# Input loaded first, parameter stage merged into the GLA stage, first norm's weight spread by a TensorE product into PSUM

## The chip, the cores and the metric

The kernel runs on one core of a Trainium2 chip. The metric is the device time of one execution in microseconds (us); the time of a kernel is the median of its runs. The engines are TensorE (PE, its weight loads PEld), VectorE (DVE), ScalarE (ACT), GpSimd (POOL) and SyncE (SP), which issues the DMAs. SBUF is the on-chip memory, PSUM the memory that TensorE writes its results to.

## What is computed

Two blocks of a language model in a row, fp32, on one sequence of 1024 rows of width 1024. The change lies in the very first steps: the first RMS norm of the input and the gate projection behind it.

```python
def first_block(x, mix_norm_w, ...):
    h = rmsnorm(x, mix_norm_w[0])
    x = x + gla_mixer(h, gla_w_in, gla_w_gate2, gla_b_gate, gla_norm_w, gla_w_out)
    h = rmsnorm(x, ffn_norm_w[0])
    x = x + conv_ffn(h, ffn_w_up, ffn_conv_w, ffn_conv_b, ffn_w_down)
    return rmsnorm(x, final_norm_w)

def second_block(x, ...):        # the output of the first block
    x = x + hybrid_mixer(rms_norm(x, norm_mix), ...)
    x = x + jnp.square(jax.nn.relu(rms_norm(x, norm_mlp) @ w_up)) @ w_down
    return rms_norm(x, norm_final)
```

rmsnorm divides each row of x by the root of its mean square and multiplies it by a weight vector of length 1024. In gla_mixer (gated linear attention, 4 heads), h is multiplied with one wide matrix that holds the keys, queries, values, the output gate and a decay gate of rank 16.

## The kernel before

The program is a sequence of stages: parameters (L902), gla (L955), gated_ffn, hybrid, square_ffn. Each ends in end_stage (L890): semaphores are cleared and all engines meet at a barrier (L893). Within a stage each engine runs its own instruction list, ordered by semaphores. fp32 products are made of three matmuls on high and low parts (product, L131): high times high, high times low, low times high. So every operand is split into two tensors.

**parameters** loads an identity matrix (L912), then 14 small tensors of per-channel parameters as rows (L914 to L933), then the 8 row tiles of x (128x1024 each, 512 KB, L936), all on SP's queue. TensorE turns the rows into columns in PSUM (L944) when all of them are there; VectorE copies them to c.par (L951) and also sets c.zero, a column of zeros. Later stages read c.par; within gla the first readers are the gate's absolute value on ACT (L1212) and its counterpart on VectorE (L1278).

**gla** starts on SP with the norm's weight row, which the load spreads over all 128 partitions into the tile gla_q (L1035), and the 128 columns of the weight matrix that hold the gate (graw, in gla_y, L1036). Then follow, in the order of a list of phases, the second gate weight (L1043) and the tiles of the wide matrix (st.load, L109), each after the first two waiting for a free raw buffer. GpSimd splits graw into high and low parts (L1063, L1066) and then each weight tile (L125, L128), into four slots; the fifth tile waits until TensorE has used a slot.

The norm (class Norm, L184) goes over the 8 tiles m, in an order that Lags (L745) writes out. ACT: square of tile k (L200), root of tile k-1 (L211), high part of tile k-4 (L238). VectorE: variance of tile k-1 (L206), scaling of tile k-2 (reciprocal L216, then L225: X times the reciprocal root times the weight row, into one of two buffers in gla_v), low part of tile k-4 (L245, from PSUM and SBUF). TensorE: turning of each scaled tile by 8 transposes (L232) into PSUM DD or MM; it waits for the scaled tile and for the low part two tiles earlier. A scaling waits for the turning two tiles earlier, and the first one for the weight row (L218).

After tile 7 TensorE makes the gate product (L1097, 48 matmuls of 128x512 into MM), ACT copies it (L1200), TensorE makes the first gate of head 0 (L1128), and then the key tile (k.0), and so on through the phases, by head.

Of the kernel before, what the change touches and what calls it, by code (L numbers as in the profile page):

```python
# [15 lines left out]
ACT = mybir.ActivationFunctionType  # L16
AX = mybir.AxisListType.X
F32 = mybir.dt.float32
# [5 lines left out]
P = 128  # L24
SEQ = 1024
D = 1024
MT = SEQ // P
DOWN = 2 * MT
KT = D // P
HALF = 512  # L30
# [7 lines left out]
FT = FFN_DIM // P  # L38
# [18 lines left out]
C_END = C_NM + 8  # L57
# [126 lines left out]
class Norm:  # L184
# [3 lines left out]
    def __init__(self, sem, name, core, xn, junk, row, pairs, ready):  # L188
        self.core, self.xn, self.junk, self.row, self.ready = core, xn, junk, row, ready
        self.pairs = pairs  # L190
        self.row_in, self.squared, self.vars, self.roots, self.scaled, self.turned, self.hi, self.lo = (
            sem(f"{name}_{s}") for s in ("row_in", "squared", "var", "root", "scaled", "turned", "hi", "lo"))
# [20 lines left out]
    def scale(self, dve, m):  # L213
# [3 lines left out]
        if m == 0:  # L217
            dve.wait_ge(self.row_in, 16)  # L218
# [512 lines left out]
class RowNorm(Norm):  # L731


    def __init__(self, sem, name, core, junk, row, ready):
        self.core, self.junk, self.row, self.ready = core, junk, row, ready
# [91 lines left out]
class Program:  # L827
# [74 lines left out]
    def parameters(self):  # L902
        nc, c, a = self.nc, self.core, self.a
        with ExitStack() as ctx:
            rows = ctx.enter_context(nc.sbuf_tensor("param_rows", [P, 3, P], F32))[:]
            s_rows, s_id, s_turn, s_par = (self.sem(n) for n in ("rows_in", "ident_in", "params_turned", "params_ready"))
            last = C_END - 2 * ROWS
            block = ctx.enter_context(nc.Block())

            @block.sync  # L910
            def _(sp):
                sp.dma_start(c.ident, a["ident"]).then_inc(s_id, 16)  # L912
                taps = a["ffn_conv_w"][0].rearrange("t (f p) -> (t f) p", p=P)
                sp.dma_start(rows[0:ROWS, 0, :], taps[0:ROWS, :]).then_inc(s_rows, 16)  # L914
                sp.dma_start(rows[0:2 * FT, 1, :], taps[ROWS:3 * 2 * FT, :]).then_inc(s_rows, 16)
                sp.dma_start(rows[2 * FT:ROWS, 1, :],
                             a["ffn_conv_b"][0].rearrange("(f p) -> f p", p=P)).then_inc(s_rows, 16)
                n = 0
                for src in (
                    a["gla_b_gate"][0].rearrange("(f p) -> f p", p=P),  # L920
                    a["gla_norm_w"][0].rearrange("(f p) -> f p", p=P),
                    a["conv_w_2"][0].rearrange("t (f p) -> (t f) p", p=P),
                    a["conv_b_2"][0].rearrange("(f p) -> f p", p=P),
                    a["b_r_2"][0].rearrange("(f p) -> f p", p=P),
                    a["b_i_2"][0].rearrange("(f p) -> f p", p=P),
                    a["lam_2"][0].rearrange("(f p) -> f p", p=P),
                    a["hg_norm_2"],
                    a["lb_logits_2"][0].rearrange("(f p) -> f p", p=P),
                    a["ffn_norm_w"][0].rearrange("(f p) -> f p", p=P),
                    a["norm_mlp_2"][0].rearrange("(f p) -> f p", p=P),  # L930
                ):
                    k = src.shape[0]
                    sp.dma_start(rows[n:n + k, 2, :], src).then_inc(s_rows, 16)  # L933
                    n += k
                for m in range(MT):
                    sp.dma_start(c.X[:, m, :], a["x"][0, m * P:(m + 1) * P, :]).then_inc(self.x_in[m], 16)  # L936

            @block.tensor
            def _(pe):
                pe.wait_ge(s_id, 16)  # L940
                pe.wait_ge(s_rows, 16 * 14)
                for g in range(3):
                    k = ROWS if g < 2 else last
                    mm = pe.transpose(c.MM[:, g * ROWS:g * ROWS + k], rows[0:k, g, :], c.ident[0:k, 0:k])  # L944
                mm.then_inc(s_turn, 1)

            @block.vector
            def _(dve):
                dve.memset(c.zero, 0.0)
                dve.wait_ge(s_turn, 1)  # L950
                dve.tensor_copy(c.par, c.MM[:, 0:C_END]).then_inc(s_par, 1)  # L951
                dve.wait_ge(s_par, 1)


    def gla(self, following):  # L955
# [6 lines left out]
        with ExitStack() as ctx:  # L962
# [26 lines left out]
            def at(h, name):  # L989
# [13 lines left out]
                "y_hi", "y_lo", "down_mm", "down_add")}  # L1003
            scratch = V.rearrange("p (b m) v -> p b (m v)", b=2)
            norm = Norm(self.sem, "gla_norm", c, scratch, T1, Q, (c.DD, c.MM), lambda m: (self.x_in[m], 16))
# [83 lines left out]
            def _(pe):  # L1089
                pe.sem_inc(st.used, 1)  # L1090
                head.tensor(pe, lambda m: None)
                pe.wait_ge(norm.lo, MT)
# [7 lines left out]
                pe.wait_ge(s["glr"], 1)  # L1100

# [95 lines left out]
            def _(act):  # L1197
# [1459 lines left out]
```

## Time and profile before

| | us |
|---|---|
| median of 3 runs | 2998.28 |
| the runs | 2997.21 to 3000.92 |
| the profiled execution | 2997.87 |
| its span in the trace | 2995.1 |
| TensorE busy | 2807.6 (94%) |
| VectorE busy | 1550.7 (52%) |
| GpSimd busy | 1624.7 (54%) |
| ACT busy | 1044.1 (35%) |

The profile is that of one execution. Its span starts with the first and ends with the last recorded instruction; the execution's own time is 2.8 us longer. Times in the rows are microseconds from the span's start unless marked ns. SPq is a DMA issue on SP. A row of the timeline gives start, duration, engine, line, operation, the tile written and the tiles read, the count of merged instructions, and in brackets how long the engine had been idle before and which event ended that. The granted clock of TensorE is given as a share of 2.4 GHz.

### The profile page before, as it was taken

The numbers are of one execution on the slowest core, as the hardware profiler recorded it, in microseconds if no ns is written. First come the engines' busy times: TensorE is split into PE (matmuls) and PEld (weight loads), VectorE is DVE, ScalarE is ACT, GpSimd is POOL, SyncE is SP. The second block draws the span as 40 slices with busy tenths as digits, with TensorE's granted clock in tenths as the row PEclk, the third lists the DMA queues.
The fourth block names the chain that finished last, engine by engine and source line by source line (L and its number), as shares of the span: only waits on it lengthen the run. The fifth ranks groups of instructions, "written<-read, shape, count | busy, mean of one in ns | idle before, by whom it ended". The sixth has DMA issues, their size and how long they took to land. (4 is left out here: it accounts for less than half of the span.)

```text
span 2995.1 us, 38841 instructions
## 1 busy us (share of the span) xinstructions
PE 2807.6 (94%) x13675; PEld 2323.1 (78%) x13675; DVE 1550.7 (52%) x1972; ACT 1044.1 (35%) x1484; POOL 1624.7 (54%) x1096
## 2 busy tenths in 40 slices
PE   5999997799999999589999999999998999999998
PEld 4888786688888887467777777777777788888886
DVE  4233425355555555846566566566444344444445
ACT  3213215333333333434444444443524222222222
POOL 3332333577677765665465465565433656555552
PEclk8999998899999999799999999999999999999999
DMA  3110110121111112111121121111250111111112
GB/s 115 36 50 28 42 42 0 35 57 54 51 49 56 56 49 70 60 46 35 54 61 33 56 60 32 57 57 36 77 190 8 50 49 56 56 56 45 46 49 84
DMA packets 200853, 160.62 MB, mean 54 GB/s; under 512 B 6246, under 2 KB 176827, under 8 KB 200763
## 3 DMA queue, kind: packets, MB, share of 16 engines
q1 hardware_dynamic: 200763, 159.35, 17.6%
q8 instruction: 64, 1.05, 0.1%
q14 instruction: 26, 0.21, 0.0%
HBM read 143.60 MB, written 15.73 MB: 53 GB/s over the span
## 5 line engine op out<-in xcount | busy, mean ns | idle before, releaser
L312 POOL TENSOR_TENSOR w_lo<-w_raw,w_hi 128x512 fp32r<-128x512 f32 x280 | 393.6, 1412 | 310.1 <-ACT w_hi L306 309.9
L408 PE MATMUL PA<-h_hi,w_hi 128*128 128x512 f32 x840 | 352.6, 420 | 61.1 <-ACT hy_gm L2338 19.9
L409 PE MATMUL PA<-h_lo,w_hi 128*128 128x512 f32 x840 | 340.1, 405 | 0.0
L410 PE MATMUL PA<-h_hi,w_lo 128*128 128x512 f32 x840 | 339.3, 404 | 0.0
L312 POOL TENSOR_TENSOR w_lo<-f_sums,w_hi 128x512 fp32r<-128x512 f32 x114 | 168.5, 1478 | 168.8 <-ACT w_hi L306 168.8
L306 ACT CAST w_hi<-w_raw 128x512 fp32r<-128x512 f32 x280 | 168.7, 616 | 245.4 <-DMA w_raw<-in_w_in 115.8
L408 PEld LDWEIGHTS PA<-h_hi,w_hi 128*128 128x128 f32 x840 | 166.0, 198 | 104.4 <-issue 35.1
L408 PE MATMUL PB<-f_t_hi,w_hi 128*128 128x512 f32 x560 | 220.9, 395 | 1.7 <-ACT hy_tm L2341 0.9
L410 PE MATMUL PB<-f_t_hi,w_lo 128*128 128x512 f32 x560 | 218.3, 390 | 0.0
L409 PE MATMUL PB<-f_t_lo,w_hi 128*128 128x512 f32 x560 | 217.9, 389 | 0.0
L312 POOL TENSOR_TENSOR w_lo<-w_lo_raw,w_hi 128x512 fp32r<-128x512 f32 x108 | 140.4, 1307 | 128.9 <-ACT w_hi L306 128.9
L409 PEld LDWEIGHTS PA<-h_lo,w_hi 128*128 128x128 f32 x840 | 166.5, 198 | 37.2 <-issue 3.6
L410 PEld LDWEIGHTS PA<-h_hi,w_lo 128*128 128x128 f32 x840 | 165.4, 197 | 36.7
L362 POOL TENSOR_TENSOR w_raw<-w_raw,params 128x1024 f32<-128x1024 f32 x76 | 143.0, 1903 | 77.1 <-DMA w_raw<-in_ffn_w_up 50.2
L312 POOL TENSOR_TENSOR w_lo<-hy_ring_sums,w_hi 128x512 fp32r<-128x512 f32 x96 | 137.2, 1429 | 70.6 <-ACT w_hi L306 70.6
L134 PE MATMUL DD<-w_hi,f_a_hi 128*128 128x512 f32 x416 | 162.9, 392 | 4.7 <-POOL w_lo L312 4.7
L135 PE MATMUL DD<-w_lo,f_a_hi 128*128 128x512 f32 x416 | 162.8, 391 | 0.0
L136 PE MATMUL DD<-w_hi,f_a_lo 128*128 128x512 f32 x416 | 162.8, 391 | 0.0
L134 PE MATMUL MM<-w_hi,f_a_hi 128*128 128x512 f32 x416 | 162.1, 390 | 0.0
L135 PE MATMUL MM<-w_lo,f_a_hi 128*128 128x512 f32 x416 | 162.0, 389 | 0.0
L136 PE MATMUL MM<-w_hi,f_a_lo 128*128 128x512 f32 x416 | 161.8, 389 | 0.0
L125 POOL TENSOR_TENSOR w_hi<-w_raw,params 128x1024 fp32r<-128x1024 f32 x24 | 48.4, 2016 | 192.3 <-PE PB L136 86.1
(469 smaller groups left out, 7139.1 us busy)
## 6 DMA issues: line engine op xcount, KB each, us to landing
w_raw<-in_w_in SPq DMA_DIRECT2D x64, 512.0 KB, 5.3
w_raw<-in_ffn_w_up SPq DMA_DIRECT2D x44, 512.0 KB, 4.6
w_raw<-in_w_up SPq DMA_DIRECT2D x32, 512.0 KB, 5.3
w_lo_raw<-in_w_down SPq DMA_DIRECT2D x64, 256.0 KB, 2.5
w_raw<-in_gla_w_in SPq DMA_DIRECT2D x24, 512.0 KB, 3.7
w_lo_raw<-in_ffn_w_down SPq DMA_DIRECT2D x44, 256.0 KB, 2.6
X<-in_x SPq DMA_DIRECT2D x8, 512.0 KB, 6.6
w_raw<-in_gla_w_out SPq DMA_DIRECT2D x8, 512.0 KB, 3.5
```

Of the source, the lines that this page charges most:

```text
L125: pool.tensor_tensor(hi, raw, self.core.zero[:, 0:1].broadcast_to([P, UNIT]), ALU.add)\
L134: pe.matmul(out, ah, bh, start=first, stop=False)
L135: pe.matmul(out, ah, bl, start=False, stop=False)
L136: return pe.matmul(out, al, bh, start=False, stop=last)
L306: act.copy(self.slot(i, p)[0], source).then_inc(self.hi_done, 1)
L312: pool.tensor_tensor(lo, source, hi.bitcast(F32), ALU.subtract).then_inc(self.split, 1)
L362: pool.tensor_tensor(raw, raw, column.unsqueeze(2).broadcast_to([P, KT, P]), ALU.mult)\
L408: pe.matmul(bank, ah[:, k, :], bh[:, k, :], start=(k == 0 and not more), stop=False, skip_group_check=more)
L409: pe.matmul(bank, ah[:, k, :], bl[:, k, :], start=False, stop=False, skip_group_check=more)
L410: mm = pe.matmul(bank, al[:, k, :], bh[:, k, :], start=False, stop=(k == 3), skip_group_check=more)
```

## The change

The stage parameters goes away, with its barrier. SP now begins, in the gla stage, with the norm's weight row as one row of 4 KB in one partition, then x tile 0, the identity, x tiles 1 to 7, graw, the 14 small parameter loads, and then the phases as before. TensorE multiplies a row of 128 ones with the weight row, in two products of 512 columns, into the PSUM tile PA; the scalings read the weight row there. The turning of the parameters stands on TensorE between the norm's turnings and the gate product, in PB; the copy to c.par stands on VectorE after the norm. ACT takes one root of a zero before anything else. TensorE and ACT wait for the copy before the first gate; GpSimd and ACT wait for the column of zeros, which VectorE now sets in this stage. T2, T3 and Q of the stage, free until later, hold the rows, the weight row and the ones.

```diff
@@ class Norm @@
         if m == 0:
-            dve.wait_ge(self.row_in, 16)
+            dve.wait_ge(*(self.row_ready or (self.row_in, 16)))
@@ parameters() becomes load_parameters(): the same 14 loads, no barrier @@
-            def _(sp):
-                sp.dma_start(c.ident, a["ident"]).then_inc(s_id, 16)
...
-                for m in range(MT):
-                    sp.dma_start(c.X[:, m, :], a["x"][0, m * P:(m + 1) * P, :]).then_inc(self.x_in[m], 16)
...
+    def load_parameters(self, sp, rows, arrived):
+        a = self.a
+        taps = a["ffn_conv_w"][0].rearrange("t (f p) -> (t f) p", p=P)
+        sp.dma_start(rows[0:ROWS, 0, :], taps[0:ROWS, :]).then_inc(arrived, 16)
...
+            k = src.shape[0]
+            sp.dma_start(rows[n:n + k, 2, :], src).then_inc(arrived, 16)
+            n += k
@@ gla, tiles @@
+            param_rows = T2[:, 0:3 * P].rearrange("p (g n) -> p g n", g=3)
+            mix_row, ones = T3[0:1, :], Q[0:1, 0:P]
-            norm = Norm(self.sem, "gla_norm", c, scratch, T1, Q, (c.DD, c.MM), lambda m: (self.x_in[m], 16))
+            norm = Norm(self.sem, "gla_norm", c, scratch, T1, c.PA, (c.DD, c.MM), lambda m: (self.x_in[m], 16))
+            norm.row_ready = s["mix_row"], 1
@@ gla, sync @@
-                sp.dma_start(norm.row, a["mix_norm_w"][0].partition_broadcast(P)).then_inc(norm.row_in, 16)
+                sp.dma_start(mix_row, a["mix_norm_w"]).then_inc(s["mix_in"], 16)
+                for m in range(MT):
+                    sp.dma_start(c.X[:, m, :], a["x"][0, m * P:(m + 1) * P, :]).then_inc(self.x_in[m], 16)
+                    if m == 0:
+                        sp.dma_start(c.ident, a["ident"]).then_inc(s["ident_in"], 16)
                 sp.dma_start(graw, W[:, :, GLA_IN - P:GLA_IN]).then_inc(s["graw_in"], 16)
+                self.load_parameters(sp, param_rows, s["rows_in"])
@@ gla, gpsimd @@
                 pool.wait_ge(s["graw_in"], 16)
+                pool.wait_ge(s["zero"], 1)
@@ gla, tensor @@
+                pe.wait_ge(s["mix_in"], 16)
+                pe.wait_ge(s["ones"], 1)
+                for half in range(2):
+                    cols = slice(half * HALF, (half + 1) * HALF)
+                    mm = pe.matmul(c.PA[:, cols], ones, mix_row[:, cols], start=True, stop=True)
+                mm.then_inc(s["mix_row"], 1)
+                pe.wait_ge(s["ident_in"], 16)
                 head.tensor(pe, lambda m: None)
+                pe.wait_ge(s["rows_in"], 16 * 14)
+                for g in range(3):
+                    k = ROWS if g < 2 else C_END - 2 * ROWS
+                    mm = pe.transpose(c.PB[:, g * ROWS:g * ROWS + k], param_rows[0:k, g, :], c.ident[0:k, 0:k])
+                mm.then_inc(s["params_turned"], 1)
                 pe.wait_ge(norm.lo, MT)
...
                 pe.wait_ge(s["glr"], 1)
+                pe.wait_ge(s["params"], 1)
@@ gla, scalar @@
+                act.wait_ge(s["zero"], 1)
+                act.activation(qo[:, 0:1], c.zero, ACT.Sqrt)
                 head.scalar(act)
                 act.wait_ge(s["glr_mm"], 1)
                 act.copy(GLR, c.MM).then_inc(s["glr"], 1)
+                act.wait_ge(s["params"], 1)
@@ gla, vector @@
+                dve.memset(ones, 1.0).then_inc(s["ones"], 1)
+                dve.memset(c.zero, 0.0).then_inc(s["zero"], 1)
...
                 head.vector(dve, lambda m: None)
+                dve.wait_ge(s["params_turned"], 1)
+                dve.tensor_copy(c.par, c.PB[:, 0:C_END]).then_inc(s["params"], 1)
+                dve.wait_ge(s["params"], 1)
@@ build @@
-        p.parameters()
-        p.end_stage()
         p.gla(stream_of("f1", p.f1_ring))
```

## Rows read from the trace of the kernel before

**Rows 1.** page, slices: TensorE's busy tenths in 40 equal slices

```profile
PE   5999997799999999589999999999998999999998
```

**Rows 2.** waits of TensorE to 110 us: waiter, releaser: total, times, longest

```profile
PE DD L232 <- DVE gla_v L225: 13.5, 1, 13.5
```

**Rows 3.** timeline from the start

```profile
0.76 0.39 SPq L912 DMA_DIRECT2D ident<-in_ident  x1
...
6.10 3.86 SPq L936 DMA_DIRECT2D X<-in_x  x8
...
7.38 0.69 PE L944 MATMUL MM<-ident,param_rows 88*128 88x88 f32 x3 [7.38 <-DMA param_rows<-in_norm_mlp]
...
10.77 0.33 SPq L1035 DMA_DIRECT2D gla_q<-in_mix_norm_w  x1
...
11.63 5.14 SPq L1043 DMA_DIRECT2D gla_gate<-in_gla_w_gate  x1
```

**Rows 4.** from issue to landing: x tiles, weight row (gla_q), identity (size, us)

```profile
DMA to landing us min/median/max: 3.7/6.6/9.3
DMA to landing us min/median/max: 9.4/9.4/9.4
ident<-in_ident SPq DMA_DIRECT2D x1, 64.0 KB, 1.9
```

**Rows 5.** timeline, first squares on ACT and first scalings on VectorE

```profile
12.07 1.06 ACT L200 ACTIVATE gla_t<-X 128x1024 f32<-128x1024 f32 x1
...
13.32 1.06 ACT L200 ACTIVATE gla_t<-X 128x1024 f32<-128x1024 f32 x1
...
20.25 1.28 DVE L225 SCALAR_TENSOR_TENSOR gla_v<-X,rs,gla_q 128x1024 f32<-128x1024 f32 x1 [4.07 <-DMA gla_q<-in_mix_norm_w]
...
23.59 2.27 DVE L225 SCALAR_TENSOR_TENSOR gla_v<-X,rs,gla_q 128x1024 f32<-128x1024 f32 x1 [0.43 <-PE DD L232]
```

**Rows 6.** timeline of the norm under way, VectorE and GpSimd

```profile
30.49 1.50 DVE L225 SCALAR_TENSOR_TENSOR gla_v<-X,rs,gla_q 128x1024 f32<-128x1024 f32 x1
30.99 3.22 POOL L128 TENSOR_TENSOR w_lo<-w_raw,w_hi 128x1024 fp32r<-128x1024 f32 x1
...
31.91 1.21 DVE L245 TENSOR_TENSOR h_lo<-DD,h_hi 128x1024 fp32r<-128x1024 f32 x1
...
33.33 1.96 DVE L225 SCALAR_TENSOR_TENSOR gla_v<-X,rs,gla_q 128x1024 f32<-128x1024 f32 x1
```

**Rows 7.** L225 grouped (busy us, mean ns); L1319 by source (ns min/median/max)

```profile
L225 DVE SCALAR_TENSOR_TENSOR gla_v<-X,rs,gla_q 128x1024 f32<-128x1024 f32 x8 | 13.8, 1720 | 4.9 <-DMA gla_q<-in_mix_norm_w 4.1 <-PE DD L232 0.4
L1319 DVE SCALAR_TENSOR_TENSOR gla_y_lo<-MM,params,gla_y_hi x6: 1275/1283/1284, 160.6 to 382.8; 128x1024 fp32r<-128x1024 f32 x6
```

**Rows 8.** timeline, GpSimd's first and last early operation, and the norm's end

```profile
21.99 2.79 POOL L1063 TENSOR_TENSOR gla_y_hi<-gla_y,params 128x1024 fp32r<-128x1024 f32 x1 [21.52 <-DMA gla_y<-in_gla_w_in]
...
39.40 2.02 DVE L225 SCALAR_TENSOR_TENSOR gla_v<-X,rs,gla_q 128x1024 f32<-128x1024 f32 x1
...
42.69 1.94 PE L232 MATMUL MM<-ident,gla_v 128*128 128x128 f32 x8 [1.35 <-DVE h_lo L245]
...
46.99 0.79 PE L134 MATMUL MM<-h_hi,gla_y_hi 128*128 128x512 f32 x1 [2.36 <-DVE h_lo L245]
...
47.52 2.38 POOL L128 TENSOR_TENSOR gla_w_lo<-w_raw,gla_w_hi 128x1024 fp32r<-128x1024 f32 x1
```

**Rows 9.** timeline behind the product; windows (busy us, PEclk, DMA share, GB/s)

```profile
61.44 1.98 PE L1128 MATMUL DD<-gla_glr,gla_gate 128*128 128x512 f32 x4 [1.10 <-ACT gla_glr L1200]
...
62.86 0.80 PE L134 MATMUL PA<-h_hi,w_hi 128*128 128x512 f32 x1
30.00:40.00 10.00, 6.42 (x27) 5.34 (x28) 9.70 (x15) 5.37 (x9) 9.84 (x4) 0.50 0.17 52
51.00:52.00 1.00, 1.00 (x4) 0.84 (x3) 0.00 (x0) 0.00 (x0) 0.00 (x0) 0.65 0.79 147
```

**Rows 10.** waits of TensorE from 62 to 500 us, the largest group

```profile
PE MM L1117 <- DVE gla_y L1273: 7.4, 4, 1.9
```

More of the change, by code:

```diff
@@ L190, in __init__ @@
         self.pairs = pairs
+        self.row_ready = None
         self.row_in, self.squared, self.vars, self.roots, self.scaled, self.turned, self.hi, self.lo = (
@@ L734, in __init__ @@
     def __init__(self, sem, name, core, junk, row, ready):
-        self.core, self.junk, self.row, self.ready = core, junk, row, ready
+        self.core, self.junk, self.row, self.ready, self.row_ready = core, junk, row, ready, None
         self.row_in, self.squared, self.vars, self.roots, self.scaled = (
@@ L900, in h_tiles @@
                 for x in (c.hhi, c.hlo)]
[L902 to L910, printed above, removed]
-            def _(sp):
-                sp.dma_start(c.ident, a["ident"]).then_inc(s_id, 16)
[L913 to L934, printed above, removed]
-                for m in range(MT):
-                    sp.dma_start(c.X[:, m, :], a["x"][0, m * P:(m + 1) * P, :]).then_inc(self.x_in[m], 16)
[L938 to L952, printed above, removed]
@@ new lines, in load_parameters @@
+    def load_parameters(self, sp, rows, arrived):
+        a = self.a
+        taps = a["ffn_conv_w"][0].rearrange("t (f p) -> (t f) p", p=P)
+        sp.dma_start(rows[0:ROWS, 0, :], taps[0:ROWS, :]).then_inc(arrived, 16)
+        sp.dma_start(rows[0:2 * FT, 1, :], taps[ROWS:3 * 2 * FT, :]).then_inc(arrived, 16)
+        sp.dma_start(rows[2 * FT:ROWS, 1, :], a["ffn_conv_b"][0].rearrange("(f p) -> f p", p=P)).then_inc(arrived, 16)
+        n = 0
+        for src in (
+            a["gla_b_gate"][0].rearrange("(f p) -> f p", p=P),
+            a["gla_norm_w"][0].rearrange("(f p) -> f p", p=P),
+            a["conv_w_2"][0].rearrange("t (f p) -> (t f) p", p=P),
+            a["conv_b_2"][0].rearrange("(f p) -> f p", p=P),
+            a["b_r_2"][0].rearrange("(f p) -> f p", p=P),
+            a["b_i_2"][0].rearrange("(f p) -> f p", p=P),
+            a["lam_2"][0].rearrange("(f p) -> f p", p=P),
+            a["hg_norm_2"],
+            a["lb_logits_2"][0].rearrange("(f p) -> f p", p=P),
+            a["ffn_norm_w"][0].rearrange("(f p) -> f p", p=P),
+            a["norm_mlp_2"][0].rearrange("(f p) -> f p", p=P),
+        ):
+            k = src.shape[0]
+            sp.dma_start(rows[n:n + k, 2, :], src).then_inc(arrived, 16)
+            n += k
@@ L1002, in gla @@
                 "r", "kdt_mm", "kdt", "st_mm", "s", "o_mm", "o_sq", "o_ms", "o_sd", "o_n", "y", "yt_mm",
-                "y_hi", "y_lo", "down_mm", "down_add")}
+                "y_hi", "y_lo", "down_mm", "down_add", "ident_in", "mix_in", "ones", "mix_row", "rows_in",
+                "params_turned", "params", "zero")}
+            param_rows = T2[:, 0:3 * P].rearrange("p (g n) -> p g n", g=3)
+            mix_row, ones = T3[0:1, :], Q[0:1, 0:P]
             scratch = V.rearrange("p (b m) v -> p b (m v)", b=2)
-            norm = Norm(self.sem, "gla_norm", c, scratch, T1, Q, (c.DD, c.MM), lambda m: (self.x_in[m], 16))
+            norm = Norm(self.sem, "gla_norm", c, scratch, T1, c.PA, (c.DD, c.MM), lambda m: (self.x_in[m], 16))
+            norm.row_ready = s["mix_row"], 1
             head = Lags(None, norm)
```

## The prediction

> **What bounds the kernel now.** I began with the shares by engine and their forty slices [rows 1]: TensorE is busy for 94% of the span and from the second slice on hardly leaves it, but the first slice (75 us) has a 5. The change touches only that slice, so everything is read there. TensorE's waits up to 110 us [rows 2] are led by 13.5 us for the first normalised tile. The start of the timeline [rows 3] shows why. SP issues the identity and 14 small parameter loads first, so the first tile of x is issued at 6.10; TensorE turns the parameters at 7.38; a barrier follows; and only at 10.77 is the norm's weight row requested, a load of 512 KB spread over all partitions, behind 4 MB of x in the same queue. It takes 9.4 us to land, a tile of x 3.7 to 9.3 us [rows 4]. So VectorE's first scaling starts at 20.25 with three tiles already squared, on the event "weight row landed" [rows 5]. From there the norm runs tile by tile on VectorE, which is full: one scaling (L225), one low half (L245) and two tiny operations each [rows 6]. The last low half releases the gate product of 48 matmuls at 46.99 [rows 8]. After that TensorE waits for nothing that keeps its own time: up to 500 us its largest group of waits sums to 7.4 us, for VectorE, and none is for a DMA or GpSimd [rows 10]. The path is therefore: load order, weight row, eight tiles on VectorE, gate product, TensorE to the end. What the product's start moves, the end moves.
>
> **Part 1, start of the chain.** SP starts at 0.76. An issue of a tile takes 3.86/8 = 0.48 us and of a small load about 0.35 (15 issues from 0.76 to 6.10) [rows 3]. After the change the order is weight row (0.76), x tile 0 (1.13), identity, x tiles 1 to 7. Tile 0 landed 3.7 us after its issue [rows 4], so now at 4.85. The last landed 9.3 us after an issue at 9.5, at 18.8; that is 1.29 us a tile. Tile 1, behind the 64 KB identity, comes at 6.3, tile 2 at 7.6, tile 7 at 14.0. ACT takes 1.25 us for a square [rows 5]: square 0 ends at 6.1, square 1 at 7.6, root 0 at 7.8. The loop lets VectorE scale tile 0 after the variance of tile 1, so at 8.05 instead of 20.25: **12.2 us earlier**. Next it waits for TensorE's turning of tile 0, as before: 20.25 to 23.59 is 3.34 us [rows 5], so the third scaling starts at 11.4.
>
> What must be there by 8.05 and is new: the weight row in PSUM. Its 4 KB load is issued at 0.76; the 64 KB identity landed 1.9 us after its issue [rows 4], so about 2.7. The two products on a row of ones are not in the trace; the nearest rows are the gate's own two fp32 products of 128x512, 1.98 us together at full clock [rows 9], at the lower clock about double. They end at 4.7 to 6.7, at least 1.3 us before they are needed: nothing on the path, and a microsecond for each that the row is late beyond that. The memset of ones and zeros are below 0.2 us each, before 2 us. ACT's root of a zero, with the table load that it brings, runs while ACT would stand idle until tile 0 lands at 4.85: nothing.
>
> **Part 2, the eight scalings.** By the grouped row they took 13.8 us, 1.72 each, though the shortest took 1.28 [rows 7]: 3.5 us of excess. The timeline says where it is. At 30.49 VectorE starts a scaling (X and weight row both in SBUF); GpSimd's operation before 30.99 is just ending; the scaling lasts 1.50. The GpSimd operation that starts at 30.99 lasts 3.22, against 2.38 when VectorE is idle, and the next scaling, from 33.33, lasts 1.96 [rows 6, 8]. The low halves, which read one operand from PSUM, take 1.21 in the same stretch [rows 6]. So two SBUF operands on VectorE and GpSimd's work wait for each other. Now the weight row is read from PSUM: 1.28 us each, the figure of the same kind of operation with one operand in PSUM, L1319 [rows 7]. Bounds: 0 us (the wait stays) to 3.5 us gained; I take **3.5 us**, because L1319 and L245 are nearest. From the third scaling on a tile then costs 2.84 - (1.50 - 1.28) = 2.62 us [rows 6]. The rest of the loop has room: TensorE turns a tile in 1.94 at the lower clock [rows 8], ACT needs about 1.0 for the high half and 1.25 for the square, 2.3 with the root. x arrives every 1.29 us, so it is not late again.
>
> The Trainium skill, page "SBUF — State Buffer", section "Who interferes with whom", says that a VectorE instruction with two SBUF inputs and a GpSimd instruction that reads SBUF exclude each other for the whole instruction, and that with at most one SBUF input there is no contention. By that rule, the trace agrees: the 3.22 and the 1.96 are each a whole wait plus an unslowed operation. The Trainium skill, page "VectorE: DVE Perf Modes", section on the TRN2 errata, speaks against the change: 120 fixed cycles with a PSUM source against 58, an estimated 0.065 us a scaling, 0.5 us in all. L1319's 1.28 us with a PSUM operand equals the scaling's 1.28 from SBUF, so the row does not bear it out and the sum leaves it out.
>
> **Part 3, the end of the norm.** Before, from the start of the eighth scaling (39.40) to the product (46.99) are 7.59 us: scaling 2.02, low half, turning 1.94, high half, low half [rows 8]. With 1.28 it is 6.85. New: third scaling 11.4, five steps of 2.62, eighth scaling 24.5, product at 31.35. Against 46.99 that is **15.6 us** earlier (12.2 + 3.5, less rounding).
>
> **Part 4, the parameters moved in behind.** SP issues the load of graw and then the 14 small ones at 0.35 us: 5.9 to 10.8, landing behind x and graw, some 5 MB at 0.41 MB/us from 3.6 on: by about 16. If the queue holds them as it held L1043's issue, 5.14 us [rows 3], by 21. TensorE waits for them after the last turning, which ends at about 28.9: its three small transposes (0.7 us, as at 7.38 [rows 3]) fit in the 2.3 us in which it waits for the last low half anyway. VectorE copies 128x277 in 0.45 us after its last low half, beside the 13 us of the product; ACT and TensorE want the result only behind the product. Cost: nothing while that cover stands, up to 0.7 + 0.45 us without it. The barrier and the old stage cost nothing more, they are inside the 20.25.
>
> Also behind the small loads are the gate weights and the first two weight tiles, 11 to 16.8. GpSimd gets graw at about 15.6 (21.99 before) and needs two halves and four weight tiles, 27.9 us in all (21.99 to 49.90 [rows 8]), less where VectorE no longer blocks it: done by 44 at the latest, by 49 if those loads are 5 us late. TensorE takes the first weight tile at about 47 instead of 62.8 [rows 9] and it is split by 27 to 32. Cost nothing; after this GpSimd waits for TensorE's slots as before.
>
> **Part 5, clock.** TensorE's granted clock was at its lower level in the second half of the norm (0.50, 1.2 GHz) and rose to the upper one (2.4 GHz) between 51 and 52 us, about 4.4 us into the product that had kept TensorE busy without a gap since 46.99 [rows 8, 9]. I expect the same: 11 matmuls at 0.43 us instead of 0.23, worth 2.2 us. It is the same cost on both sides. Bounds: the clock is already high (2.2 us gained) or rises later, by about as much lost.
>
> **Sum.** Profiled execution: span 2995.1, time 2997.87. Less 15.6: span 2979.5, time 2982.3. The median of the runs shown is 0.4 us above the profiled one: **2982.7 us**.
>
> **Rivals.**
> (a) The wait between VectorE and GpSimd stays although the row is in PSUM, or PSUM operands are slower: 2 to 3.5 us less gain, 2984.7 to 2986.2. For: the trace has no operation with exactly the second operand in PSUM beside a busy GpSimd. Against: L245 under the same GpSimd stretch.
> (b) The chain's start is later than I say: the row's load plus two products at the lower clock, or a slower first landing in a cold queue. 1 to 4 us less gain, 2983.7 to 2986.7.
> (c) The clock stays high into the product, since the turnings are now closer together: 2.2 us more, 2980.5.
> (d) Slower: the small parameter loads. TensorE stands in order in front of the product until all 14 have landed. If SP's queue, full of 4.6 MB, held each as long as L1043's load, 5.14 us, they would land near 80 and the product would start 33 us later than before: 3031 us. It costs from a landing at about 29 on, makes the kernel no faster from 46.3, and slower by over 0.2% from 52.3. Against: the eight x tiles were issued without any such hold [rows 3] and data drain by 16.
> (e) The gain is absorbed: a queue half as bad, landing at 40 to 52, gives within 0.2%.
>
> **Chances.** Forecast 0.62, own range 2980.0 to 2984.7; (a) 0.10; (b) 0.13; (c) 0.07; other faster outcomes 0.02; (e) 0.04; (d) 0.02. A measurement of this kernel tells about 0.2%, 6 us, from no change. Faster 0.94, same 0.04, slower 0.02. The range leaves out (d), (e) and half of the extremes: 2979.5 to 2988.
>
> **What would show it.** Right: first scaling near 8, eight scalings at 1.28 us, product near 31.3, no wait of TensorE for parameters, GpSimd's four early weight operations near 1.9 and 2.4 us, and from the product on the old timeline shifted by 15 to 16 us. Wrong: a first scaling released by the weight row in PSUM (b); scalings near 1.7 (a); TensorE waiting for a parameter load (d, e); a different granted clock in the product (c); a new TensorE wait for GpSimd behind 47 us.

## The result, and the profile after the change

The changed kernel takes 2979.56 us (median of 4 runs, 2976.03 to 2984.49) against 2998.9 us (4 runs, 2997.21 to 3000.92); the ratio is 0.994, 95% interval 0.9925 to 0.9954. In two further comparisons the same kernel gave 2980.30 us against 2999.03 us, ratio 0.9943 (0.9929 to 0.9956), and 2981.78 us against 2996.86 us, ratio 0.9953 (0.9939 to 0.9966). Over all 14 runs its median is 2980.3 us. The profiled execution is the slowest of its four: 2984.49 us, span 2982.7.

TensorE's slices now begin with a 7, where before they began with a 5 [rows 1]; of the other 39 digits one has changed, by one.

```profile
PE   7999997899999999589999999999998999999998
```

The start of the timeline after the change. The product on ones (L1078) answers to the load of the weight row [rows 3], L226 is the scaling that was L225 [rows 5 and 6], L1046 and L1049 are GpSimd's splitting of graw [rows 8].

```profile
2.20 3.77 PE L1078 MATMUL PA<-gla_t,gla_q 1*128 1x512 f32 x4 [2.20 <-DMA gla_t<-in_mix_norm_w]
...
6.96 5.17 SPq L907 DMA_DIRECT2D gla_t<-in_ffn_conv_w  x1
7.74 1.06 ACT L201 ACTIVATE gla_t<-X 128x1024 f32<-128x1024 f32 x1 [1.77 <-DMA X<-in_x]
...
9.25 1.28 DVE L226 SCALAR_TENSOR_TENSOR gla_v<-X,rs,PA 128x1024 f32<-128x1024 f32 x1
...
12.66 1.28 DVE L226 SCALAR_TENSOR_TENSOR gla_v<-X,rs,PA 128x1024 f32<-128x1024 f32 x1 [0.51 <-PE DD L233]
...
15.28 1.28 DVE L226 SCALAR_TENSOR_TENSOR gla_v<-X,rs,PA 128x1024 f32<-128x1024 f32 x1
...
17.37 1.89 POOL L1046 TENSOR_TENSOR gla_y_hi<-gla_y,params 128x1024 fp32r<-128x1024 f32 x1 [16.91 <-DMA gla_y<-in_gla_w_in]
...
19.34 2.36 POOL L1049 TENSOR_TENSOR gla_y_lo<-gla_y,gla_y_hi 128x1024 fp32r<-128x1024 f32 x1
```

What to see: the weight row is in PSUM at 5.97 (2.20 plus 3.77) and nobody waits for it. The first scaling starts at 9.25 instead of 20.25, directly behind square and root of tile 1, which ACT could start only at 7.74 because x tile 1 had not landed. Every scaling takes 1.28 us, and GpSimd's operations take 1.89 and 2.36 us beside them. SP is held for 5.17 us at the first small load.

The end of the norm and the product, with rows that answer to [rows 8 and 9]:

```profile
25.69 1.28 DVE L226 SCALAR_TENSOR_TENSOR gla_v<-X,rs,PA 128x1024 f32<-128x1024 f32 x1
...
28.26 1.94 PE L233 MATMUL MM<-ident,gla_v 128*128 128x128 f32 x8 [0.62 <-DVE h_lo L246]
...
29.99 0.67 PE L1085 MATMUL PB<-ident,gla_t 88*128 88x88 f32 x3
...
32.42 0.44 DVE L1256 COPY params<-PB 128x277 f32<-128x277 f32 x1
...
32.56 0.79 PE L134 MATMUL MM<-h_hi,gla_y_hi 128*128 128x512 f32 x1 [1.90 <-DVE h_lo L246]
...
38.27 0.48 PE L135 MATMUL MM<-h_lo,gla_y_hi 128*128 128x512 f32 x1
...
46.50 1.01 ACT L1198 COPY gla_glr<-MM 128x1024 f32<-128x1024 f32 x1 [15.25 <-PE MM L136]
...
48.98 0.80 PE L134 MATMUL PA<-h_hi,w_hi 128*128 128x512 f32 x1
```

The product starts at 32.56 (before 46.99: 14.4 us earlier), the copy behind it at 46.50 (before 60.38: 13.9 us earlier), the first key tile at 48.98 (before 62.86: 13.9). The three transposes of the parameters lie inside the wait for the last low half, and the copy of the parameters beside the product's first matmuls. TensorE's waits up to 110 us, to be read beside [rows 2]: the 13.5 us for the first scaled tile are 4.7, and no row names a parameter load.

```profile
PE DD L233 <- DVE gla_v L226: 4.7, 1, 4.7
...
PE PA L1078 <- DMA gla_t<-in_mix_norm_w: 2.2, 1, 2.2
```

### The profile page after: what moved, and what is told of

It reads as the page before. It is cut to its first block and busy times, and to the rows that moved or that the text cites. A ratio compares the mean times of both kernels' runs of the same rounds, so it can differ in the third digit from the quotient of the medians.

```text
span 2982.7 us, 38829 instructions
## 1 busy us (share of the span) xinstructions
PE 2813.7 (94%) x13679; PEld 2325.7 (78%) x13679; DVE 1545.7 (52%) x1973; ACT 1042.7 (35%) x1484; POOL 1619.8 (54%) x1096
## 3 DMA queue, kind: packets, MB, share of 16 engines
q1 hardware_dynamic: 200621, 158.83, 17.6%
```

## The experiments

In all of them the gate product's start and the start of ACT's copy behind it are read as the two marks of the path (46.99 and 60.38 in the kernel before, 32.56 and 46.50 in the changed one). Kernels are compared with runs of the kernel before on the same chip.

### The changed kernel again

No edit.

> The changed kernel once more, nothing edited. It is to separate the change from the spread between executions. Theory (the start alone moved): gate product starts at 32 to 33 us, as in the changed kernel's profile (32.56), and any difference in the whole time lies in single stretches of lower granted clock in the GLA heads (there were three of 3.4 us up to 400 us in the changed kernel's profile, one in the profile of before). Median 2977 to 2983. Rival (something later waits for a weight or a parameter): the same extra TensorE waits in every execution at the same place, median near 2984.

Measured: 2980.30 us (5 runs, 2979.64 to 2985.21), ratio 0.9943 (0.9929 to 0.9956). Product at 32.35, copy at 45.76. The profiled execution has a span of 2977.9, 4.8 us less than the first one of the same kernel, though its copy starts only 0.7 us earlier. Windows of TensorE in the three places where the first execution had fallen to the lower clock (columns: the window and its length, busy us and counts of PE, PEld, DVE, ACT, POOL, then the granted clock, the DMA share and GB/s), first of that execution, then of this one:

```profile
120.00:135.00 15.00, 13.09 (x76) 8.90 (x75) 7.57 (x22) 5.78 (x15) 7.30 (x4) 0.89 0.09 34
228.00:246.00 18.00, 16.18 (x92) 11.03 (x89) 10.30 (x22) 8.39 (x17) 9.34 (x4) 0.91 0.10 30
340.00:357.00 17.00, 15.18 (x77) 10.16 (x76) 10.90 (x18) 10.09 (x16) 9.34 (x4) 0.90 0.17 47
```

```profile
120.00:135.00 15.00, 13.10 (x81) 9.54 (x80) 8.26 (x21) 7.98 (x15) 8.04 (x4) 1.00 0.10 35
228.00:246.00 18.00, 16.17 (x85) 11.23 (x84) 11.32 (x20) 10.60 (x18) 9.34 (x4) 0.91 0.17 46
340.00:357.00 17.00, 15.19 (x79) 11.39 (x78) 12.84 (x20) 12.13 (x16) 9.37 (x4) 1.00 0.21 62
```

The clock is below 1.00 in three windows there and in one here. These are stretches of 3.4 us at 1.2 GHz. In the first execution they start at 130.6, 239.8 and 349.1 us, one head (109 us) apart, each within 1.1 us of the end of a wait of TensorE for VectorE of 1.8 to 1.9 us. The second execution has the same three waits, but only one such stretch, at 238.4. Summed over the record of the granted clock behind 60 us, TensorE was at the lower clock for 181.5 us in the first execution and for 174.7 in this one. At half the clock a busy engine loses half of the time, so I take half of the 6.8 us, 3.4, as an estimate; with the 0.7 us of the start this makes 4.1 of the 4.8. TensorE's large waits behind 62 us are the same in both (7.4 us for L1277's result in the one and 7.3 in the other), so nothing new is late.

### The weight row read from SBUF

```diff
-            norm = Norm(..., scratch, T1, c.PA, (c.DD, c.MM), ...)
-            norm.row_ready = s["mix_row"], 1
+            norm = Norm(..., scratch, T1, Q, (c.DD, c.MM), ...)
+            norm.row_ready = s["row_copied"], 1
@@ vector, ahead of the norm @@
+                dve.wait_ge(s["mix_row"], 1)
+                dve.tensor_copy(Q, c.PA).then_inc(s["row_copied"], 1)
```

> The changed kernel, but VectorE first copies the spread weight row from PSUM to SBUF, and the scalings read it there. Theory (VectorE with two SBUF operands and GpSimd exclude each other): the scalings before GpSimd's first operation (17.4 us) stay at 1.28 us, the four after it take 1.5 to 2.0, GpSimd's early operations 2.9 and 3.2 instead of 1.9 and 2.4; product starts 2 to 3 us later than 32.6, at 34.5 to 35.6. Rival (PSUM has nothing to do with it; the earlier start alone avoids GpSimd): eight scalings at 1.28 and the product at 32.6 as in the changed kernel.

```profile
17.19 2.48 DVE L226 SCALAR_TENSOR_TENSOR gla_v<-X,rs,gla_q 128x1024 f32<-128x1024 f32 x1
...
18.67 3.22 POOL L1049 TENSOR_TENSOR gla_y_lo<-gla_y,gla_y_hi 128x1024 fp32r<-128x1024 f32 x1
...
21.02 1.96 DVE L226 SCALAR_TENSOR_TENSOR gla_v<-X,rs,gla_q 128x1024 f32<-128x1024 f32 x1
...
34.68 0.79 PE L134 MATMUL MM<-h_hi,gla_y_hi 128*128 128x512 f32 x1 [1.90 <-DVE h_lo L246]
```

Measured: 2985.15 us (4 runs, 2984.47 to 2985.54), ratio 0.9952 (0.9937 to 0.9967). Four scalings at 1.28 us, then, from GpSimd's first operation at 16.70 on, 2.48, 1.96, 1.50 and 2.02; product at 34.68. The 2.48 is above the 1.5 to 2.0 that I expected, and GpSimd's first operation took 1.89 and not 2.9: it had begun before the fifth scaling, which waited for it. The first scaling was early here (7.82), so the stretch from it to the product is the fair measure: 26.86 us against 23.31 in the first profile of the changed kernel and 24.05 in the second. The 2.84 us over four scalings (7.96 less 4 times 1.28) lie on the path. The rival, that the earlier start alone avoids GpSimd, is out: it does so for the first four tiles only.

### The weight row as a spreading load, behind x

```diff
-                sp.dma_start(mix_row, a["mix_norm_w"]).then_inc(s["mix_in"], 16)
@@ behind the eight x tiles @@
+                sp.dma_start(norm.row, a["mix_norm_w"][0].partition_broadcast(P)).then_inc(norm.row_in, 16)
@@ tensor @@
-                (the wait for mix_in and ones, and the two products)
```

> The changed kernel, but without the product on ones: the weight row comes again as a load that spreads it over 128 partitions (512 KB), behind the eight x tiles. Theory (the first scaling waited for this load, x alone gives little): first scaling at 15.5 to 17 us, released by that load; scalings again 1.28 to 2.3 us beside GpSimd; product at 41.5 to 43.5 us; total 4 to 6 us under the kernel before. Rival (x's early arrival is the gain, the row only rides along): first scaling near 9.3, product near 35, total 10 or more us under the kernel before.

```profile
15.99 1.28 DVE L226 SCALAR_TENSOR_TENSOR gla_v<-X,rs,gla_q 128x1024 f32<-128x1024 f32 x1 [7.93 <-DMA gla_q<-in_mix_norm_w]
...
42.75 0.80 PE L134 MATMUL MM<-h_hi,gla_y_hi 128*128 128x512 f32 x1 [1.90 <-DVE h_lo L246]
```

Measured: 2993.69 us (10 runs, 2988.40 to 2997.84), ratio 0.9987 (0.9977 to 0.9996). The edit also takes the scalings' weight row back into SBUF. VectorE stood idle for 7.93 us until the row landed at 16; the scalings were 1.28 to 2.20 us again; product at 42.75, 4.2 us earlier than before. With x first and the stages merged, but the row in its old form and place, most of the gain is missing. A spreading load issued ahead of x, with no product on TensorE, was not tried.

### The weight row alone

The kernel before with the 4 KB load in the old place, the product on ones, and the scalings from PSUM; the parameter stage stays.

```diff
-                sp.dma_start(norm.row, a["mix_norm_w"][0].partition_broadcast(P)).then_inc(norm.row_in, 16)
+                sp.dma_start(mix_row, a["mix_norm_w"]).then_inc(s["mix_in"], 16)
@@ tensor, ahead of the norm @@
+                (the two products into PA, as in the change)
```

> The kernel before with one part of the change: the weight row is a 4 KB load, spread by the product on ones into PSUM and read there; the parameter stage, its barrier and the load order stay. Theory (the row's place behind x decides when it comes, its size hardly): it lands with the last x tile near 19, TensorE needs 3.4 to 3.8 us for the two products at the lower clock, first scaling at 22 to 23, but eight scalings at 1.28 us, product at 45.5 to 46.5, total 0 to 2 us under the kernel before. Rival (the spreading load of 512 KB is what delays the first scaling): first scaling at 15 to 18, product at 38 to 42, total 5 to 9 us under it.

```profile
18.62 3.78 PE L1098 MATMUL PA<-gla_t,gla_q 1*128 1x512 f32 x4 [10.60 <-DMA gla_t<-in_mix_norm_w]
...
22.52 1.28 DVE L226 SCALAR_TENSOR_TENSOR gla_v<-X,rs,PA 128x1024 f32<-128x1024 f32 x1 [6.31 <-PE PA L1098]
...
45.61 0.50 PE L134 MATMUL MM<-h_hi,gla_y_hi 128*128 128x512 f32 x1 [2.36 <-DVE h_lo L246]
```

Measured: 2995.45 us (10 runs, 2988.34 to 2996.85), ratio 0.9989 (0.9979 to 0.9998). The 4 KB, requested at 10.80, landed at 18.6 with the last of x; TensorE then took 3.78 us for the two products, so the first scaling is 2.3 us later than before. The eight scalings at 1.28 us win it back and 1.4 us more, although GpSimd works beside them from 20.56 on. The median fell by 3.7 us against the kernel before on its chip, more than the 0 to 2 that I expected; the profiled execution fell by 1.8. The size of the row's load matters little, its place in the queue much: in this place 4 KB took 7.8 us to land and 512 KB took 9.4 [rows 4], at the front 4 KB took 1.44.

### x first, with two stages

```diff
@@ parameters() @@
+                for m in range(MT):
+                    sp.dma_start(c.X[:, m, :], a["x"][0, m * P:(m + 1) * P, :]).then_inc(self.x_in[m], 16)
                 sp.dma_start(c.ident, a["ident"]).then_inc(s_id, 16)
...
-                for m in range(MT):
-                    sp.dma_start(c.X[:, m, :], a["x"][0, m * P:(m + 1) * P, :]).then_inc(self.x_in[m], 16)
```

> The kernel before with the x tiles issued ahead of the identity and the 14 small loads, still in a stage of its own with its barrier, and the weight row as before. Theory (the stages must be merged for x first to pay): the stage now ends only when the small loads have landed behind x, near 18 to 21, the barrier adds 2.2, the spread row is requested after it and lands about 3 us later, first scaling at 24 to 28, product at 50 to 54, total 3 to 7 us above the kernel before. Rival (x early is worth most of the gain by itself): first scaling before 16, total at least 4 us under the kernel before.

```profile
16.12 0.69 PE L944 MATMUL MM<-ident,param_rows 88*128 88x88 f32 x3 [16.12 <-DMA param_rows<-in_norm_mlp]
...
18.20 0.36 SPq L1035 DMA_DIRECT2D gla_q<-in_mix_norm_w  x1
...
23.69 1.28 DVE L225 SCALAR_TENSOR_TENSOR gla_v<-X,rs,gla_q 128x1024 f32<-128x1024 f32 x1
...
51.78 0.80 PE L134 MATMUL MM<-h_hi,gla_y_hi 128*128 128x512 f32 x1 [2.36 <-DVE h_lo L245]
```

Measured: 3003.63 us (10 runs, 2995.44 to 3007.85), ratio 1.0013 (1.0004 to 1.0023). This has x first as in the change, but neither its merge nor its weight row, and it is slower. TensorE waits until 16.12 for the small loads, now behind x; the row is requested at 18.20; the first scaling starts at 23.69 and the product at 51.78, 4.8 us later than before. First scaling (forecast 24 to 28) a little better, product (50 to 54) as forecast. Against the run with the spreading load behind x, which has x first, that load and the merge, the product is 9.0 us later (51.78 against 42.75): that is what the merge is worth once x is first. The merge without x first was not run.

### The small loads ahead of x

```diff
                 sp.dma_start(mix_row, a["mix_norm_w"]).then_inc(s["mix_in"], 16)
+                self.load_parameters(sp, param_rows, s["rows_in"])
                 for m in range(MT):
...
-                self.load_parameters(sp, param_rows, s["rows_in"])
```

> The changed kernel, but the 14 small parameter loads are issued first, ahead of the weight row and x, with nothing else moved. Theory (load order): everything starts later by the issue of 14 loads, 4.7 to 5.2 us; first scaling at 13.5 to 14.5, product at 37 to 38, total about 5 us above the changed kernel. Rival (the slow second x tile and SP's 5.17 us hold in the changed kernel come from its order, and this order avoids them): first scaling at 12.5 to 13, product at 35.5 to 36.5, 3 to 4 us above.

```profile
6.01 0.36 SPq L1015 DMA_DIRECT2D X<-in_x  x1
...
10.95 5.20 SPq L1025 DMA_DIRECT2D gla_gate<-in_gla_w_gate  x1
...
12.68 1.28 DVE L226 SCALAR_TENSOR_TENSOR gla_v<-X,rs,PA 128x1024 f32<-128x1024 f32 x1
...
36.94 0.79 PE L134 MATMUL MM<-h_hi,gla_y_hi 128*128 128x512 f32 x1 [1.90 <-DVE h_lo L246]
```

The small loads stand ahead of x, but behind the weight row, which stays first; the expectation has it otherwise.

Measured: 2986.82 us (4 runs, 2985.02 to 2991.73), ratio 0.9961 (0.9946 to 0.9976). x tile 0 is issued 4.84 us later, the product starts 4.4 and 4.6 us later than in the two profiles of the changed kernel. The numbers lie between the two forecasts: the first scaling at 12.68 falls into the rival's range, because tile 1 came nearly in time here; the product lies between the two ranges, next to the theory's; the total is 6.5 us above the changed kernel's, which is nearer to the theory. SP's hold of 5.20 us did not go away, it moved to the next issue behind graw. As an experiment on tile 1 this one decides nothing; the next does.

### The identity behind tile 2

```diff
-                    if m == 0:
+                    if m == 2:
                         sp.dma_start(c.ident, a["ident"]).then_inc(s["ident_in"], 16)
```

> The changed kernel, but the identity is issued behind x tile 2 instead of tile 0. In three profiles of the changed kernel and its variants x tiles 1 or 2 came 0.3 to 1.8 us late. Theory (the first packets of a cold queue are slow whatever they carry): tiles 1 or 2 are late again, first scaling at 7.8 to 9.3, total within 1 us of the changed kernel. Rival (the identity's 512-byte rows hold up tile 1): tile 1 lands by 6.3, first scaling at 7.6 to 7.9, product at 31 to 31.6.

```profile
5.96 1.06 ACT L201 ACTIVATE gla_t<-X 128x1024 f32<-128x1024 f32 x1
...
7.48 1.28 DVE L226 SCALAR_TENSOR_TENSOR gla_v<-X,rs,PA 128x1024 f32<-128x1024 f32 x1
...
10.89 1.28 DVE L226 SCALAR_TENSOR_TENSOR gla_v<-X,rs,PA 128x1024 f32<-128x1024 f32 x1 [0.50 <-PE DD L233]
...
30.89 0.79 PE L134 MATMUL MM<-h_hi,gla_y_hi 128*128 128x512 f32 x1 [1.90 <-DVE h_lo L246]
```

My theory fell here. The numbers are a little better even than the rival's (7.6 to 7.9 and 31 to 31.6). ACT goes from tile 0 to 1 to 2 without a wait, the first scaling is at 7.48, the third at 10.89, the product at 30.89. In the DMA records of this execution no packet of x behind the first tile's took over 0.35 us; in those of the changed kernel's three executions 18, 24 and 9 did, up to 1.6 us against the usual 0.16. So the identity's place holds up tiles 1 and 2; whether it does so by its short rows of 512 bytes was not tested apart. Measured in whole: 2982.91 us (4 runs, 2978.56 to 2985.43), ratio 0.9952 (0.9937 to 0.9967). So the 1.5 us at the start are not to be seen in so few runs.

### The gate product begun early

The product's first half needs the columns of tiles 0 to 3 only. It is begun while TensorE would wait.

```diff
-                head.tensor(pe, lambda m: None)
+                for m in range(MT):
+                    norm.turn(pe, m)
+                    if m == 5:
+                        pe.wait_ge(norm.lo, 4)
+                        pe.wait_ge(s["g_lo"], 1)
+                        gate_part(0, (0,))
+                    if m == 6:
+                        gate_part(0, (1,))
@@ behind the parameters' transposes, which now go to PA @@
+                gate_part(0, range(2, KT))
                 pe.wait_ge(norm.lo, MT)
+                mm = gate_part(1, range(KT))
```

gate_part(half, ks) makes the three matmuls of each k for one half of the columns, into PB.

> The changed kernel, and in addition the gate product's first half, whose columns need only tiles 0 to 3, is begun during the norm: 3 of its 24 matmuls behind turning 5, 3 behind turning 6, the other 18 behind the parameters' transposes, while TensorE waited for the last low half; it is written to PB, the turned parameters to PA. Theory (TensorE's waits between turnings and the slow clock at the product's start are now what is left on the path): TensorE works without a gap from 25 us, its clock rises by about 30 to 32, the second half starts near 36, the product is complete at 42 to 43.5 instead of 46.2 to 46.5, total 3 to 4.5 us under the changed kernel. Rival (the norm's chain on VectorE is delayed by the inserted matmuls as much as they win): last low half later than 33.5, product complete at 45.5 or later, no difference.

```profile
24.48 0.78 PE L134 MATMUL PB<-h_hi,gla_y_hi 128*128 128x512 f32 x1
...
27.72 0.39 PE L135 MATMUL PB<-h_lo,gla_y_hi 128*128 128x512 f32 x1
...
39.08 1.01 ACT L1208 COPY gla_glr<-PB 128x1024 f32<-128x1024 f32 x1 [8.82 <-PE PB L136]
```

Measured: 2979.11 us (5 runs, 2973.04 to 2980.03), ratio 0.9931 (0.9917 to 0.9944). The mark moved by more than I expected, to 39.08: 6.7 to 7.4 us before the changed kernel's. The matmuls are at the upper clock (0.23 us apart) from 27.7 on, so only three of the product's 48 ran slowly where 13 and 10 had; at 0.20 us each that is 1.4 to 2.0 us of the gain. The last low half was not delayed, it came at 30.30, 0.8 to 1.0 us earlier, since the last turning too was at the upper clock (1.04 us instead of 1.94). The rest is the work done while TensorE had waited. But the profiled span, 2977.1, is only 0.8 us below that of the changed kernel's second execution: this execution had the three low stretches at 123, 232 and 341 us and 187.2 us at the lower clock in all, 12.5 more than that one. Half of it, 6.2 us, is about what is missing.

### Early product again, with the later identity, and the changed kernel beside them

> The kernel with the gate product begun early once more, nothing edited, for the spread between executions and a second trace. Its first profile had the product complete 7.4 us before the changed kernel's, but TensorE was at the lower clock for 187 us behind 60 us, against 175, and its median was only 1.2 us lower. Theory (the whole time is the start's shift plus half of the difference in time at the lower clock, and which stretches are low is a matter of the single execution): total in profile within 2 us of that sum, median 2974 to 2979. Rival (the earlier start lands on the low stretches each time): three low stretches up to 350 us again and a median near 2979.

> The gate product begun early and the identity behind x tile 2, both edits together. Theory (an identity load behind tile 0 holds up tiles 1 and 2, worth about 1 us): first scaling at 7.5, third at 10.9, product complete at 37.5 to 38.3 instead of 39.0, and all x packets but the first ones at their usual 0.16 us. Rival (the on-time tiles of the one profile with a later identity were chance): third scaling again at 11.5 or later.

> The changed kernel a third time, nothing edited, on the chip of the two others, for their comparison. Theory: product at 32 to 33, median 2978 to 2983; in the profile, against the kernel before, total = start's shift plus half of the difference in time at the lower clock, within 2 us. Rival (the changed kernel itself falls on the low stretches more often): median above 2983.

The three expectations are for the early product again, for the kernel with both edits, and for the changed kernel a third time. All three ran on one chip, where the kernel before took 2996.86 us (9 runs). The start of ACT's copy, first of the early product again, then with the later identity:

```profile
38.67 1.01 ACT L1208 COPY gla_glr<-PB 128x1024 f32<-128x1024 f32 x1 [8.81 <-PE PB L136]
```

```profile
7.58 1.28 DVE L226 SCALAR_TENSOR_TENSOR gla_v<-X,rs,PA 128x1024 f32<-128x1024 f32 x1
...
10.99 1.28 DVE L226 SCALAR_TENSOR_TENSOR gla_v<-X,rs,PA 128x1024 f32<-128x1024 f32 x1 [0.50 <-PE DD L233]
...
38.25 1.01 ACT L1208 COPY gla_glr<-PB 128x1024 f32<-128x1024 f32 x1 [8.80 <-PE PB L136]
```

| kernel | median us (5 runs) | range | ratio, 95% interval |
|---|---|---|---|
| changed kernel | 2981.78 | 2979.03 to 2986.48 | 0.9953, 0.9939 to 0.9966 |
| product begun early | 2976.91 | 2973.29 to 2980.51 | 0.9934, 0.9920 to 0.9948 |
| with the later identity | 2974.14 | 2971.87 to 2979.44 | 0.9925, 0.9912 to 0.9939 |

The changed kernel had its product at 32 to 33 again (copy at 46.05) and a first scaling at 9.26. The later identity gave the first scaling at 7.58 and the third at 10.99, and 2 slow packets instead of 12, so the one profile was no chance; the copy at 38.25 is 0.4 us earlier than without it, as forecast at the edge of the range. The last kernel is the fastest of all: 2974.14 us, 22.7 us below the kernel before on its chip and 7.6 below the changed one. Its interval overlaps that of the early product alone, so the 2.8 us between these two are not shown.

The sum "shift of the copy's start plus half of the difference in time at the lower clock" against the profiled execution of before (copy 60.38, lower clock for 181.6 us behind 60 us, in 124.7 of them TensorE busy, span 2995.1). The last two columns have the part of the low stretches in which TensorE was busy, and the sum with half of the difference in that part alone:

| execution | copy at | lower clock us | sum | measured | busy at it | sum by busy part |
|---|---|---|---|---|---|---|
| changed kernel, first | 46.50 | 181.5 | 13.9 | 12.4 | 128.9 | 11.8 |
| changed kernel, second | 45.76 | 174.7 | 18.1 | 17.2 | 117.7 | 18.1 |
| changed kernel, third | 46.05 | 174.9 | 17.7 | 16.9 | 118.3 | 17.5 |
| row from SBUF | 48.42 | 180.4 | 12.6 | 12.0 | 128.1 | 10.3 |
| spreading load behind x | 56.02 | 174.9 | 7.7 | 7.1 | 117.8 | 7.8 |
| row alone | 58.45 | 184.5 | 0.5 | 1.8 | 125.8 | 1.4 |
| x first, two stages | 64.66 | 191.3 | -9.1 | -7.1 | 131.1 | -7.5 |
| small loads first | 49.55 | 178.7 | 12.3 | 10.9 | 124.9 | 10.8 |
| later identity | 44.42 | 174.8 | 19.4 | 18.3 | 119.0 | 18.8 |
| product early, first | 39.08 | 187.2 | 18.5 | 18.0 | 133.3 | 17.0 |
| product early, second | 38.67 | 180.2 | 22.4 | 20.0 | 127.3 | 20.4 |
| early and later identity | 38.25 | 194.7 | 15.6 | 18.3 | 133.7 | 17.6 |

Ten of the twelve are within 2 us; the last two miss by 2.4 and 2.7. Only two of the twelve had the 2 us on record beforehand: the changed kernel's third execution held it, the early product's second missed it. The traces give a likely reason: TensorE is not busy in all of a low stretch, and where it waits there is nothing for the lower clock to cost. Two low stretches of the last kernel, one full and one mostly waiting (TensorE busy for 3.40 of 3.40 us, and for 11.91 of 27.20):

```profile
341.20:344.60 3.40, 3.40 (x7) 1.67 (x6) 2.90 (x5) 0.65 (x2) 3.32 (x3) 0.51 0.54 154
1218.20:1245.40 27.20, 11.91 (x53) 10.83 (x54) 25.04 (x35) 13.56 (x27) 15.94 (x10) 0.50 0.11 42
```

With the busy part alone the two misses shrink to 0.4 and 0.7 and eleven of the twelve are within 1.1 us; the row from SBUF does worse, 1.7 off instead of 0.6. This sum was made up after the runs and has not been put to a new one. Whether the start's place draws certain low stretches, or each execution its own, stays open. The three kernels with the early product had three, two and three of them between 100 and 350 us, and 127.3 to 133.7 us of busy time at the lower clock; the three executions of the changed kernel had three, one and one, and 117.7 to 128.9 us. So the rival, that the earlier start lands on more of them, is not out.

## Why the prediction was right, point by point

The forecast was 2982.7 us with a range to 2979.5; the measured 2979.56 lies at its lower edge, 14 runs give 2980.3.

- **The path from the load order to the first scaling** was read rightly from [rows 3 to 5]. Each link shows: the row behind x leaves VectorE idle for 7.9 us ahead of the first scaling, two stages instead of one cost 9.0 us at the product with x first and the spreading row in both, the small loads ahead of x 4.4 to 4.6 us. Single edits do little: x first alone is 4.8 us slower at the product, the row alone 1.4 us faster; x first and merged without the row is 4.2 us faster, all together 14.4. The merge alone was not run.
- **The mis-sized term of the sum** is x tile 1, put at 6.3 by a landing rate of 1.29 us a tile. It came at 7.74, the first scaling at 9.25 instead of 8.05 (8.30 in the second profile), and the third at 12.66 instead of 11.4. I took the rate from a stretch of the trace with x alone in the queue and counted the identity by its bytes. The identity behind tile 0 slowed tiles 1 and 2, as the run with the later identity shows (first scaling at 7.48, third at 10.89). In its effect this was rival (b), at 1.2 us; but both of the causes that (b) names were absent, as the weight row was ready in time and tile 0 had landed by 4.82.
- **The weight row's price**: 1.44 us to land after its issue, 3.77 us for the products, near the upper bound (double the gate's 1.98). Ready at 5.97, within the 4.7 to 6.7 forecast, and free as said.
- **The scalings**: 3.5 us for eight at 1.28 us held to the last digit; 2.62 us a tile (12.66 to 15.28); 6.87 us from the eighth scaling to the product, forecast 6.85. Rival (a) is out: the scalings beside GpSimd took 1.28 us in the changed kernel and with the row alone, and 1.50 to 2.48 with the row from SBUF. The Trainium skill, page "SBUF — State Buffer", section "Who interferes with whom", has it that two SBUF inputs on VectorE and a reading GpSimd exclude each other whole; the trace agrees: in the run with the row from SBUF GpSimd's 3.22 us are its usual 2.36 plus 0.86, in which the scaling from 17.19 to 19.67 was still under way.
- **The parameters** cost nothing, inside a wait of 1.9 us; SP's hold of 5.17 us came as foreseen from [rows 3], and rivals (d) and (e) did not come: the last small load was issued at 16.35, and the transposes at 29.99 did not wait for it.
- **The clock**: 13 slow matmuls at the product's start where 10 had been (the prediction counts 11, the last of them already faster), 0.5 us lost, inside the bound of 2.2. Rival (c) did not come.
- **The sum** of 15.6 us was 14.4 at the product and 13.9 behind it. The median fell by 19.3, 18.7 and 15.1 us in the three comparisons. What goes beyond 13.9 is within their noise: the interval of the second one, 5 runs against 15, reaches from 13.2 to 21.3 us, and the two others hold 13.9 as well. No trace shows a further step that gained. The profile of before had 6.9 us more at the lower clock than two of the three of the changed kernel, worth 3.4 us; with one trace of before, I can't say whether that is usual for it. The forecast's hit on the total is so in part luck: the start gave 1.7 us less than forecast, and the medians fell by more than the start gave.

## What to carry to other kernels

Before moving a load to the front, follow all that stands between it and its first use: here three edits paid little until they stood together, and one of them alone made the kernel slower. A small load's landing goes more by its place in the queue than by its size (1.44 us for 4 KB at the front, 7.8 behind 4 MB), and a small load put between large ones is to be costed by what it does to its neighbours. Where a product of many matmuls waits for the last of several tiles, look whether its first part needs only the first tiles: here this gave 6.7 to 7.4 us at the product's end, and 4.9 us in the medians of the two kernels on one chip.

## What the runs showed of the hardware

- The granted clock of a window reads 1.00 up to the first rise on record, though TensorE is at the lower clock until then. In the run with the spreading load that rise is at 47.2 us. A matmul before it (the next one started 0.42 us later, as at 1.2 GHz; 0.23 us is the upper clock's) and the two windows around it:

```profile
43.77 0.63 PE L136 MATMUL MM<-h_hi,gla_y_lo 128*128 128x512 f32 x1
...
40.00:45.00 5.00, 3.10 (x10) 2.38 (x9) 1.58 (x2) 1.01 (x1) 4.92 (x3) 1.00 0.39 108
45.00:50.00 5.00, 5.00 (x19) 3.98 (x18) 0.00 (x0) 0.00 (x0) 0.64 (x1) 1.00 0.37 105
```

  The same holds for the changed kernel: its first two turnings took 1.94 and 1.92 us, the third, behind the first rise at 14.6 us, 1.07. The pitch of the matmuls is the surer sign. So the two products on ones, at 2.20 us, will have run at the lower clock too, which their 3.77 us against the gate's 1.98 bear out and the column doesn't show.
- SP was held for 3.6 to 5.6 us at the issue behind graw, a load with rows of 512 bytes, in every kernel in which x was still in the queue: at the gate weight before, at the first small load after. With the queue empty (x first, two stages) the same issue took 0.56 us.
- Low stretches of the clock can repeat with the loop: 130.6, 239.8 and 349.1 us in one execution, one head (109 us) apart; two others of the same kernel have only the middle one. The shift of the copy's start plus half of the difference in TensorE's busy time at the lower clock gives the change in the span to within 1.1 us in eleven traces of twelve (1.7 in the other). The runs of one kernel lie up to 12 us apart (x first, two stages), and two traces of the same kernel by 4.8 us with equal work.
